# Constants queued behind the first weights, key columns with signals of their own, and a copy placed inside local attention's exponentials

## The reference

```python
x = x + (rms(retention(q, k, v)) * silu(gate)) @ w_out         # layer a: proj = rmsnorm(x) @ w_in, 12 groups of 512
kv = rmsnorm(x, kv_norm_g) @ w_kv                              # 256 outputs: the shared keys and values
x = x + (local_attention(q, k, v, bias, sinks) * silu(gate)) @ w_out   # layer b: window 128, 16 heads, 2 key heads
x = attention_and_experts(x, c, ada_w, ...)                    # layers c and d: two kinds of attention, 16384 experts
```

## Time and profile before

| | us |
|---|---|
| median of 3 runs | 2076.67 (2074.51 to 2078.03) |
| profiled execution, its own time | 2078.76 |
| its span, first to last instruction | 2077.0 |
| PE busy | 1986.8 (96%) |
| DVE busy | 1439.4 (69%) |
| POOL busy | 887.0 (43%) |
| ACT busy | 474.4 (23%) |
| TensorE clock granted, mean | 0.989 |

### The profile page before, as it was taken

The page is one execution under the profiler, slowest core; times in us unless marked ns, Lnnn a source line. Parts: engine busy times, 40 slices in busy tenths (PEclk is TensorE's granted clock), DMA queues, the critical chain, the costliest instruction groups (busy, mean ns, idle before and its releaser), DMA issues.

```text
span 2077.0 us, 27535 instructions
## 1 busy us (share of the span) xinstructions
PE 1986.8 (96%) x10152; PEld 1465.9 (71%) x10152; DVE 1439.4 (69%) x3091; ACT 474.4 (23%) x994; POOL 887.0 (43%) x653
## 2 busy tenths in 40 slices
PE   7999999999999999999989999999999999999996
PEld 6888876878788885688876666666666666666663
DVE  3673034333362586647999999899989999887766
ACT  4122223123552424722222010100101010010100
POOL 4354432428303652422524555445555544453332
PEclk9999999999999999999999999999999999999998
DMA  9565422515201311114348999999999999999997
GB/s 250 166 215 195 146 82 98 196 41 172 92 1 44 110 59 51 42 61 146 130 176 338 421 421 422 421 421 419 422 407 421 415 418 406 420 419 415 422 421 227
DMA packets 92627, 527.08 MB, mean 254 GB/s; under 512 B 10048, under 2 KB 14576, under 8 KB 42992
## 3 DMA queue, kind: packets, MB, share of 16 engines
q0 software_dynamic: 37440, 270.55, 32.0%
q1 hardware_dynamic: 49680, 246.95, 31.7%
q10 hardware_dynamic: 5408, 8.34, 1.9%
HBM read 518.46 MB, written 7.34 MB: 253 GB/s over the span
## 4 chain that ended last, share of the span: by engine, by line
PE 46%; DMA 27%; DVE 17%; POOL 5%; issue 3%; ACT 1%; SPq 0%; POOLq 0%; DVEq 0%; ACTq 0%
PE ps L812 28%; DMA work<-in_peer_uv,consts 14%; DMA ring<-in_peer_uv,consts 12%; PE ps L1100 5%; DVE tables L1977 3%; PE ps L840 2%; POOL work L2520 2%; DVE ring L1952 2%; DVE work L1952 2%; POOL ring L2520 2%; PE ps L898 2%; PE ps L764 1%; DVE hT L1977 1%; PE ps L955 1%; PE ps L887 1%
## 5 line engine op out<-in xcount | busy, mean ns | idle before, releaser
L1190 PE MATMUL ps<-work,tmp 128*128 128x512 f32 x1008 | 448.7, 598 | 27.6 <-DVE tmp L2002 27.4
L1165 PE MATMUL ps<-hT,work 128*128 128x256 f32 x2048 | 465.9, 381 | 0.0
L2439 POOL TENSOR_TENSOR w_lo<-ring,w_hi 128x1024 fp32r<-128x1024 f32 (+2 forms) x116 | 274.0, 2367 | 400.8 <-ACT w_hi L2070 400.7
L1165 PEld LDWEIGHTS ps<-hT,work 128*128 128x128 f32 x2048 | 384.5, 190 | 76.5 <-issue 29.6
L1190 PEld LDWEIGHTS ps<-work,tmp 128*128 128x128 f32 x1008 | 190.2, 191 | 252.6 <-issue 215.2
L2520 POOL DMA_INDIRECT work<-in_peer_uv,consts x128 | 229.8, 1795 | 268.0 <-DVE tables L1977 217.3
L2520 POOL DMA_INDIRECT ring<-in_peer_uv,consts x128 | 234.5, 1832 | 255.9 <-DVE tables L1977 227.8
L812 PE MATMUL ps<-w_hi,x_hi 128*128 128x512 f32 (+2 forms) x544 | 208.5, 384 | 1.6 <-DVE tmp L1527 1.1
L2070 ACT ACTIVATE w_hi<-ring 128x1024 fp32r<-128x1024 f32 (+2 forms) x116 | 120.5, 1042 | 386.8 <-PE ps L812 279.9
L812 PE MATMUL ps<-w_lo,x_hi 128*128 128x512 f32 (+2 forms) x544 | 207.2, 381 | 0.0
L1952 DVE CUSTOM_DVE_ANT_0 ring<-ring,tables 128x1024 f32<-128x1024 f32 x128 | 155.2, 1221 | 46.8 <-DMA ring<-in_peer_uv,consts 45.7
(11 more groups left out here) (339 smaller groups left out, 3059.1 us busy)
## 6 DMA issues: line engine op xcount, KB each, us to landing
work<-in_u_steps SPq DMA_DIRECT2D x64, 1024.0 KB
work<-in_peer_v SPq DMA_DIRECT2D x64, 1024.0 KB
ring<-in_a_w_in SPq DMA_DIRECT2D x48, 512.0 KB, 4.5
ring<-in_ada_w SPq DMA_DIRECT2D x48, 512.0 KB, 4.9
ring<-in_peer_w_q SPq DMA_DIRECT2D x32, 512.0 KB, 3.4
ring<-in_a_w_out SPq DMA_DIRECT2D x16, 512.0 KB, 4.1
ring<-in_b_w_in SPq DMA_DIRECT2D x16, 512.0 KB, 4.1
ring<-in_c_in SPq DMA_DIRECT2D x12, 512.0 KB, 3.6
```

The costliest lines, as they stand in the source:

```text
L1165: mm = pe.matmul(ps[:, 4 + s, j * DT:(j + 1) * DT], u_ring[:, s, j, k, :], hT[:, k, GATHERED * P:T], start=(k == 0), stop=(k == KD - 1))
L1190: mm = pe.matmul(ps[:, 2 * t + half, :], tmp[:, s, j * DT + t * P:j * DT + (t + 1) * P], v_ring[:, s, j, half * BANK:(half + 1) * BANK], s ...
L2439: pool.tensor_tensor(w_lo[q % NPIECE][:, 0:n], ring[:, at:at + n], w_hi[q % NPIECE][:, 0:n], ALU.subtract).then_inc(w_split, 1)
```

## The change

Three independent edits:

1. *Constants and bias.* The seven tables move from ACT's queue to SP's, behind the four pieces of group 0. The bias product on PE moves from before group 0 to just before group 1, and its bank from 0 to the one that comes next there (bank 5). DVE's two bias operations move behind the rotation of n = 0. ACT's issue of the copy to DRAM moves into its loop, at n = 2, behind the high parts up to piece (3, 2). ACT's high part of piece (0, 3) moves behind the fourth `x_hi`.
2. *Key columns.* `b_kvT` gets two semaphores; PE's products for keys and values wait on them and no longer on `x_lo`. The order of the columns is 0, 2, 4, 6, 1, 3, 5, 7 on ACT, and DVE makes all its even columns before `x_lo` of column 1.
3. *Local attention.* ACT does four exponentials of v, the copy of pair 1 of v - 1, the other four exponentials, then the copy of pair 3 of v - 1.

```diff
+KV_ORDER = (0, 2, 4, 6, 1, 3, 5, 7)
...
-    jobs.add("bias", 0)
+    jobs.skip(1)
     for n in range(12):
+        if n == 1:
+            jobs.put(jobs.turn % NB, "bias", 0)
...
                 if name == ("a_in", 1, 0):
+                    sp.dma_start(bias_w, ins["rel_bias"]).then_inc(row_loaded, 16)
...
                     if ready is not None and t == 0:
-                        drained(pe, ready, k)
+                        pe.wait_ge(ready[k % 2], k // 2 + 1)
...
             for n in range(12):
+                if n == 1:
+                    o = start("bias", 0)
+                    pe.wait_ge(row_loaded, 16 * 7)
+                    end(pe.matmul(o[0:SWA_H, 0:384], bias_w, bias_hot, start=True, stop=True), "bias", 0)
...
+                if n == 0:
+                    o = full(dve, "bias", 0)
+                    dve.wait_ge(row_loaded, 16 * 7)
+                    dve.tensor_tensor(bias_mask, o[0:SWA_H, 0:384], bias_mask, ALU.add).then_inc(bias_done, 1)
+                    dve.wait_ge(bias_done, 1)
+                    taken(dve.tensor_scalar(bias_mask, bias_mask, float(SWA_D ** 0.5), None, ALU.mult), "bias", 0)
                 if 1 <= n <= ADA_IN_A:
                     ada(n - 1)
...
+            kv_column(0)
             for k in range(KD):
+                if k == 1:
+                    for even in range(2, KD, 2):
+                        kv_column(even)
                 o = full(dve, "xT_b", k)
-                dve.wait_ge(x_high, KD + k + 1)
-                if k % 2 == 0:
-                    dve.tensor_scalar(b_kvT[:, k, :], o, col("kv_g", k), None, ALU.mult)
+                dve.wait_ge(x_high, KD + KV_ORDER.index(k) + 1)
...
-            high_parts(NPIECE)
+            high_parts(NPIECE - 1)
             for k in range(KD):
+                if k == KD // 2:
+                    high_parts(NPIECE)
...
             for n in range(12):
                 high_parts_for("a_in", n, 3)
+                if n == 2:
+                    keep_bias()
...
-            for k in range(KD):
+            for k in KV_ORDER:
                 o = full(act, "xT_b", k)
-                if k % 2:
-                    act.activation(b_kvT[:, k, :], o, ACT.Copy, scale=col("kv_g", k))
                 act.activation(x_hi[:, k, :], o, ACT.Copy, scale=col("b_g", k)).then_inc(x_high, 1)
+                if k % 2 == 0:
+                    o = full(act, "xT_b", k + 1)
+                    act.activation(b_kvT[:, k + 1, :], o, ACT.Copy, scale=col("kv_g", k + 1)).then_inc(kv_odd, 1)
...
                 for h in range(2 * SWA_JOBS):
+                    if h == SWA_JOBS:
+                        between()
...
-            for v in range(2, SWA_UNITS + SWA_PT):
-                for i in range(1, SWA_JOBS, 2):
-                    swa_kept(v - SWA_PT, i)
-                if v < SWA_UNITS:
-                    swa_exps(v)
+            for i in range(1, SWA_JOBS, 2):
+                swa_kept(0, i)
+            for v in range(2, SWA_UNITS):
+                swa_exps(v, lambda: swa_kept(v - 1, 1))
+                swa_kept(v - 1, 3)
+            for i in range(1, SWA_JOBS, 2):
+                swa_kept(SWA_UNITS - 1, i)
```

More of the change, by code:

```diff
@@ L562, in network @@
         bias_done = sem("bias_done")
+        kv_even = sem("kv_even")
+        kv_odd = sem("kv_odd")
         k_sq = sem("k_sq")
@@ L681, in _ @@
                 if name == ("a_in", 1, 0):
+                    sp.dma_start(bias_w, ins["rel_bias"]).then_inc(row_loaded, 16)
+                    sp.dma_start(bias_hot, ins["bias_hot"]).then_inc(row_loaded, 16)
+                    sp.dma_start(bias_mask, ins["bias_mask"]).then_inc(row_loaded, 16)
+                    sp.dma_start(rows[:], ins["rows"]).then_inc(row_loaded, 16)
+                    sp.dma_start(iota[:], ins["iota"]).then_inc(row_loaded, 16)
+                    sp.dma_start(trig[:], ins["trig"]).then_inc(row_loaded, 16)
+                    sp.dma_start(causal, ins["causal"]).then_inc(row_loaded, 16)
                     sp.dma_start(trigA, ins["trig_a"]).then_inc(ret_loaded, 16)
@@ L870, in _ @@
             stream_transposes("xT_a", a_xn, 0)
-            o = start("bias", 0)
-            pe.wait_ge(row_loaded, 16 * 7)
-            end(pe.matmul(o[0:SWA_H, 0:384], bias_w, bias_hot, start=True, stop=True), "bias", 0)
             pe.wait_ge(made, 1)
             for n in range(12):
+                if n == 1:
+                    o = start("bias", 0)
+                    pe.wait_ge(row_loaded, 16 * 7)
+                    end(pe.matmul(o[0:SWA_H, 0:384], bias_w, bias_hot, start=True, stop=True), "bias", 0)
                 project([("a_in", n, i) for i in range(4)], [("a_in", n, p) for p in range(4)],
@@ L911, in _ @@
             for t in range(NT):
-                tokens_by_features(("kv", t), b_kvT, lambda k: raw("kv", 0, k // 4)[:, k % 4, :], KD, 0, 256, t, "xT_b")
+                tokens_by_features(("kv", t), b_kvT, lambda k: raw("kv", 0, k // 4)[:, k % 4, :], KD, 0, 256, t, (kv_even, kv_odd))
             def swa_input(n):
@@ L1301, in _ @@
                                                ALU.subtract), "xT_a", k)
[L1302 to L1307, removed]
             dve.wait_ge(silu_c, 1)
@@ L1361, in _, with kv_column @@
                 ada_out(ADA_IN_A + n)
+            def kv_column(k):
+                o = full(dve, "xT_b", k)
+                dve.wait_ge(x_high, KD + KV_ORDER.index(k) + 1)
+                dve.tensor_scalar(b_kvT[:, k, :], o, col("kv_g", k), None, ALU.mult).then_inc(kv_even, 1)
+            kv_column(0)
             for k in range(KD):
+                if k == 1:
+                    for even in range(2, KD, 2):
+                        kv_column(even)
                 o = full(dve, "xT_b", k)
-                dve.wait_ge(x_high, KD + k + 1)
-                if k % 2 == 0:
-                    dve.tensor_scalar(b_kvT[:, k, :], o, col("kv_g", k), None, ALU.mult)
+                dve.wait_ge(x_high, KD + KV_ORDER.index(k) + 1)
                 taken(dve.scalar_tensor_tensor(x_lo["b"][:, k, :], o, col("b_g", k), x_hi[:, k, :], ALU.mult,
@@ L2048, in _ @@
         def _(act):
[L2050 to L2056, removed]
             split_n = [0]
@@ L2090, in _, with keep_bias @@
             act.activation(csil[:], col("c", 0, KD), ACT.Silu).then_inc(silu_c, 1)
-            drained(act, "bias", 0)
-            act.dma_start(ins["bias_rows"].rearrange("p h u -> h p u"),
-                          bias_mask.unsqueeze(1).to_broadcast([SWA_H, P, 384])).then_inc(bias_kept, 16)
+            def keep_bias():
+                drained(act, "bias", 0)
+                act.dma_start(ins["bias_rows"].rearrange("p h u -> h p u"),
+                              bias_mask.unsqueeze(1).to_broadcast([SWA_H, P, 384])).then_inc(bias_kept, 16)
             for n in range(12):
                 high_parts_for("a_in", n, 3)
+                if n == 2:
+                    keep_bias()
                 for t in range(NT) if n >= RET_H else ():
@@ L2165, in swa_kept, with swa_exps @@
                 taken(act.activation(dst[:, :, c0:SWA_W], src[:, :, c0:SWA_W], ACT.Copy), "swa_pT", v, i)
-            def swa_exps(v):
+            def swa_exps(v, between=lambda: None):
                 m_, d_, l_, es_ = (swa_stat(a, v) for a in range(4))
```

## The result

| | before | after |
|---|---|---|
| median, us | 2075.81 (4 runs) | 2092.97 (3 runs) |
| ratio, 95% interval | | 1.0078 [1.0065, 1.0091] |
| profiled execution, its own time | 2078.76 | 2094.24 |
| its span | 2077.0 | 2092.3 |
| TensorE clock granted, mean | 0.989 | 0.986 |

The changed kernel is 0.8% slower, 16 to 17 us; the profiled execution 15.5. Forecast were 2092.8 and +16.1. A fourth execution of the changed kernel took 8659.08 us, in a slow state that nothing here explains, and is left out. The page's slices of PE (52 us each) show where the time went: the third, 105 to 157 us, falls from 9 to 7 tenths against the earlier trace rows, and the first and the last by one tenth each.

A forecast was written before the change was run, and what follows sets the result against it. PE was taken to bound the kernel nearly everywhere. Layer a +24.5, keys and values -4.3 and local attention -4.1 summed to +16.1 us on the median 2076.67, giving 2092.8; range 2083 to 2103.

The forecast's parts named there:

- group 0 earlier: Start of layer a: tables leave ACT's queue, x comes 2.7 us sooner, group 0 starts 2.9 earlier; bounds 1 to 3.5.
- bank wait: group 1 later: Before group 1, PE stands 5.2 us until DVE takes the bias from bank 5; group 1 begins 3.1 us later.
- low clock in group 1: After PE's idle gap before group 1 the clock falls for one spell, losing 3.4 us; bounds 0 to 3.4.
- copy issued, landed: Bias copy to DRAM: issued at 97.1 behind piece (3, 2), takes 36 us, ends at 133.1; bounds 32 to 39.
- where PE stands: Group 4: DVE's rotation of n = 3 waits for the copy, so PE starts piece (4, 3) 24.5 us later.
- load beside the copy: Group 3's last piece: its load, slowed by the copy, comes about 7 us late, hidden inside DVE's wait.
- edit 2: Keys and values: products start 0.9 us earlier and the clock stays up, giving back 3.4; -4.3, bounds -0.9 to -4.7.
- edit 3: Local attention, turn 3: PE goes on 2.1 us sooner, the clock staying up gives about 2; -4.1, bounds 0 to -4.3.
- Rival (a): Layer a: the copy is quick, so only +6.5 there; total -1.9 (2074.8) or -5.3 (2071.4), not slower; chance 0.08.
- (b): Rival at group 1's wait: the clock stays up there, 3.4 us less, 2089; chance 0.14.
- (c): Rival in key/value products and local attention: the clock falls all the same, gains only 0.9 + 2.1, 2098; chance 0.15.
- (d): Rival at piece (4, 3): PE waits again and the clock falls, or the copy takes 39 us; 2096 to 2099; chance 0.13.

The follow-up runs named there:

- the copy early: The changed kernel with ACT issuing the bias copy to DRAM at n = 0 instead of n = 2; 2075.78 us, ratio 0.999.
- wide: The changed kernel with the bias replicated on 128 partitions, each writing one eighth of what its head's partition wrote, still at n = 2; 2077.74 us, ratio 1.0005.
- natural column order: The kernel before plus the key column signals and the local attention change, columns kept in order 0 to 7 on ACT and DVE; 2070.55 us, ratio 0.9968.

## Why the prediction was right

It was right in the total (+16.1, measured 15.5 profiled and 17.2 between the medians), in the order of the terms and in the cause, the late copy. The way in which the copy reaches PE it had wrong, and that the total fits all the same is in part luck. By its own steps:

| step | forecast | measured |
|---|---|---|
| group 0 earlier | 2.9 | 1.0 |
| bank wait: group 1 later | 3.1 | 5.0 |
| low clock in group 1 | 3.4 | 2.2 |
| copy issued, landed | 97.1, 133.1 | 96.45, 130.45 |
| where PE stands | group 4, bank wait | group 3, load of its last piece |
| load beside the copy | 14.6 | 19.8 |
| layer a | +24.5 | +23.4 |
| edit 2 | -4.3 | -4.0; -3.3 alone |
| edit 3 | -4.1 | -5.1; -5.1 alone |

- *Start: mis-sized.* The step "x, its transposes and the first `x_hi` 2.7 us earlier" took the 1.00 MB out at the full rate. In the first 9.2 us the core moved 2.61 MB before (1.66 of weights and x, 0.95 of tables) and 2.29 after: without ACT's queue the remaining one moved more than before, but 0.63 and not 0.95 MB more. x's third tile, on which the transposes hang, is squared at 9.13 in place of 10.37, 1.2 us sooner. The bias product's 0.8 us, of which 0.2 was booked, was lost fully: PE waits 1.3 us for `x_hi` and the bank of column 1 there. The lower bound given, 1, is what came.
- *Bank wait: right in mechanism and length.* From the rotation's start to group 1 it was 47.86 - 39.42 = 8.4 us, forecast 45.95 - 37.5 = 8.45; only its start carried the error of the step before.
- *Low clock: half too large.* At piece (3, 2) the delay was 6.9 us and at the rotation of n = 1 it was 7.3 (69.38 against 62.12), so the clock cost 2.2 on top of 5.0. The sum of the first three terms was forecast as 6.5: measured it is 7.3, with the start's error of 1.9 and the clock's of 1.2 going opposite ways.
- *The copy: right in place, length and price, and for the greater part wrong in the way it reaches PE.* The step that failed is "that lies inside the same wait": the late load of group 3's last piece was put at 7 us, from one load of 14.6; it took 19.8, because the weights' queue moved nothing for the first 13 of them, and PE stood 15.1 us for it, in group 3. The wait in group 4, from which the +24.5 was worked out, did not come. By the forecast's path DVE would have gone on at 133.1; it went on at 131.40, because PE's group 3 was late, with the copy already in at 130.45. The two ways have different ends, the load's landing at 122.49 and the copy's at 130.45; that they price layer a within about 1 us of each other is luck. The two were not tested apart: with the copy early or wide both are gone, and no run takes out the wait for `bias_kept` and keeps the slow copy. By the two traces it would change little: in after that wait ended 0.95 us before PE's release, and with the copy alone moved it ended last on DVE and PE did not stand for it.
- *Edit 2: right in size, one cause wrong.* "PE starts at 447.2, 0.9 earlier" failed: PE still starts 2.46 us behind the first `x_hi`, behind `x_lo` of column 0. The first tile of the products takes the bank of transposed column 0, and `start` waits until `x_lo` has read it; the new signals don't touch that. All of the gain is the time without waits after it, and the clock.
- *Edit 3: mis-sized by 1.* The wait fell by 2.1 as forecast; the rest of the stage, in which the clock now stays up, gave 3 where 2 was taken.

Rival (a) fell: the copy was slow. The likely cause is its 16 source partitions, which no view of before shows as such; with 128 it took 10.9 us. The Trainium skill's rule named beside that rival ("DMA: Bandwidth & Descriptors", Specifications: line rate from 512 B on) is thereby not refuted: it says nothing of partitions, and the 425 GB/s taken with it is a figure for 128 partitions. The estimate of 8 us from it is near the wide copy's time. Rivals (b) and (c) fell by the windows above; (d) did not occur.

## What to carry to other kernels

A transfer that nobody waits for is not free: it takes shares of the engines from the loads beside it. Ask of each moved transfer what loads run beside it in the new place, with how much slack, and not only who waits for its own end. The store from 16 partitions held the engines three times as long as the same bytes from 128. And a signal of its own for an operand does not bring the first product forward as long as the product's output bank waits for the same instruction.

## What was unexpected of the hardware

- A 3 MB store with 16 source partitions took 34.0 us (33.5 to 34.9 in all eleven kernels that have it), with 128 partitions and the same 2064 packets 10.9, and 13.6 in another place.
- While the narrow store ran, a load of 0.5 MB took up to 19.8 us, against 4.7 without it, though the core moved only 100 GB/s for the first two thirds of that time, and nothing of it was the load's.
- Stretches with not very different idle time had different granted clocks. In stretches of 6 us PE was idle for 2.4 us (after, 466 to 472), or for 2.0 and then 1.7 (natural column order), and the clock stayed at 1.00; with 2.7 us idle in 6 (before) it fell to 0.50. It fell as well after single gaps of 2.7, 3.1 and 5.1 us.
- DVE's scaling of 16x384 took 0.35 us alone and 2.20 beside POOL's subtraction, and ended 0.2 us after it; the operation just before it, reading PSUM, took its usual 0.55.
